# Mixer of a hybrid trunk: x turned on the host, and decay rows spread over the partitions through DRAM

## What is computed

```python
def rms_norm(x, g):
    return x * lax.rsqrt(jnp.mean(x * x, axis=-1, keepdims=True) + RMS_EPS) * g

def attn_ssd_mixer(h, ...):            # h = rms_norm(x, mix_norm_g)
    proj = h @ w_in                    # 1024 x 2312
    q, k, v, z, xbc, dt = split(proj)  # 512, 128, 128, 512, 1024, 8 columns
    q, k = rms_norm(q, q_norm_g), rms_norm(k, k_norm_g)          # by head of 64
    y_attn = sliding_window_sink_attention(q, k, v, sinks)       # window 128, 8 heads
    y_ssm = mamba2_heads(z, xbc, dt, ...)                        # 8 heads
    return concatenate([y_attn, y_ssm]) @ w_out

# inside mamba2_heads: xbc = silu(causal conv of 4 taps), then in chunks of 128 tokens
a_cum = jnp.cumsum(dt * a_coef, axis=2)                 # 128 tokens x 8 heads
seg = a_cum[:, :, :, None] - a_cum[:, :, None, :]       # needs a_cum along both axes
decay = jnp.exp(jnp.where(tril, seg, -jnp.inf))
y_diag = einsum(cb * decay, x * dt)
```

## Time and profile before

| | us |
|---|---|
| three runs | 2082.68, 2100.13, 2100.52 |
| median of them | 2100.13 |
| the profiled execution | 2083.14 |
| its span, first to last instruction | 2081.3 |
| the mixer in it, to the last `project_part` | about 514 |

### The profile page before, as it was taken

How to read it: one execution, slowest core, us unless ns; L and a number is a source line. 1 busy time by engine, 2 the same in 40 slices (tenths; PEclk the granted TensorE clock), 3 DMA queues, 4 the chain that set the end, 5 groups by cost and what they waited for, 6 DMA issues and landing times. The chain is left out here.

```text
span 2081.3 us, 47130 instructions
## 1 busy us (share of the span) xinstructions
PE 1879.5 (90%) x20636; PEld 1153.3 (55%) x20636; DVE 882.7 (42%) x1980; ACT 429.2 (21%) x965; POOL 427.1 (21%) x546
## 2 busy tenths in 40 slices
PE   7899999998699998898969999799969999898992
PEld 5666667664566655555635444345546665555651
DVE  2665565565721111111116899893271111111114
ACT  3332322234311110110114122143411111010110
POOL 2111100111222332222213011120222232221220
PEclk9999999999799999999989999899979999999996
DMA  9100000030699999999968455512289999999996
GB/s 312 37 1 1 1 0 0 0 122 17 254 377 423 422 424 426 425 425 425 421 250 254 100 110 127 121 31 81 81 326 401 416 424 424 428 422 424 423 390 257
DMA packets 89992, 520.60 MB, mean 250 GB/s; under 512 B 23062, under 2 KB 46666, under 8 KB 72384
## 3 DMA queue, kind: packets, MB, share of 16 engines
q1 hardware_dynamic: 63976, 457.76, 53.7%
q0 software_dynamic: 24064, 51.45, 9.0%
q10 hardware_dynamic: 1752, 8.44, 1.0%
HBM read 491.31 MB, written 34.65 MB: 253 GB/s over the span
## 5 line engine op out<-in xcount | busy, mean ns | idle before, releaser
L1367 PE MATMUL ps<-wgu,xT 128*32 128x256 f32 x7168 | 419.0, 387 | 35.1 <-issue 35.1
L1532 DVE TENSOR_TENSOR hh<-sg,ps 128x128 f32<-128x128 f32 x168 | 66.5, 396 | 704.5 <-ACT sg L1189 704.1
L1367 PEld LDWEIGHTS ps<-wgu,xT 128*32 128x32 f32 x7168 | 238.7, 112 | 192.2 <-issue 56.6
L1252 POOL DMA_INDIRECT y_rows<-my,yidx x168 | 166.6, 992 | 736.5 <-ACT my L1183 729.2
L1367 PE MATMUL ps<-early_gu,xT 128*32 128x256 f32 x3584 | 213.3, 392 | 14.9 <-issue 12.3
L1382 PE MATMUL ps<-wd,hhT 128*32 128x256 f32 x3584 | 213.8, 379 | 0.0
L1189 ACT ACTIVATE sg<-ps 128x128 f32<-128x128 f32 x168 | 46.6, 277 | 687.1 <-PE ps L1367 687.1
L1367 PEld LDWEIGHTS ps<-early_gu,xT 128*32 128x32 f32 x3584 | 118.9, 113 | 97.5 <-issue 27.7
L1382 PEld LDWEIGHTS ps<-wd,hhT 128*32 128x32 f32 x3584 | 119.6, 110 | 73.8
L2098 DVE SCALAR_TENSOR_TENSOR conv<-dd,par,conv 128x256 f32<-128x256 f32 (+1 forms) x255 | 131.5, 593 | 0.2
L787 PE MATMUL ps<-hn,early_gu 128*128 128x128 f32 x1024 | 116.8, 275 | 0.0
(11 more groups left out here) (344 smaller groups left out, 2110.9 us busy)
## 6 DMA issues: line engine op xcount, KB each, us to landing
wgu<-in_moe_w_gate_up SPq DMA_DIRECT2D x42, 4096.0 KB, 31.6
early_gu<-in_moe_w_gate_up SPq DMA_DIRECT2D x22, 4096.0 KB, 30.8
wd<-in_moe_w_down SPq DMA_DIRECT2D x42, 2048.0 KB, 29.9
early_wd<-in_moe_w_down SPq DMA_DIRECT2D x22, 2048.0 KB, 29.0
early_wd<-in_conv_w_pw SPq DMA_DIRECT2D x22, 512.0 KB, 5.5
conv<-prod POOLq DMA_DIRECT2D x20, 512.0 KB, 4.5
h_rows<-wgu ACTq DMA_DIRECT2D x8, 1024.0 KB, 3.9
early_gu<-in_w_in SPq DMA_DIRECT2D x2, 2048.0 KB, 16.7
```

What stands on the lines that cost most here:

```text
L1252: pool.indirect_dma_start(out=y_quarters, out_offset=bass.IndirectOffsetOnAxis(ap=yidx[:, tl, q:q + 1], axis=0), in_=y[:, n % YB, :], in_o ...
L1367: mm = pe.matmul(ps[TB * g:TB * g + TB, GU + n % 2, 0:2 * P].rearrange("p (a f) -> p a f", a=2), xT[:, q % 2, j, TB * tl:TB * tl + TB], wg ...
L1532: tt(hh[:, n % 2, :].rearrange("q (k f) -> q k f", k=KF), by_k(sg[:, n % 2, :]), by_k(ps[:, GU + n % 2, P:2 * P]), ALU.mult).then_inc(hh_r ...
```

## The change

- The host passes x turned (`x_turned`, 8 tiles of [128 channels, 8, 128 tokens]) beside x, and the gains and convolution weights already turned (`mixer_rows`). SyncE loads one turned tile (0.5 MB) per turn into `xT`, one buffer.
- For tiles 0 and 1 VectorE multiplies `xT` by the gain (`scale_first`); for tiles 2 to 7 GpSimd does (after `xde`, before `qk_rstd_and_dt`, turns 0 to 5). VectorE's `normalise` multiplies by `rstd` along the free axis, straight from SBUF into `hT`. `turn_hn` and `hT_evacuate` are gone.
- `rstd` along the free axis: for tiles 0 and 1 by a transpose of a repeated column (`turn_rstd`); for tiles 2 to 7 by a store of [128, 6] to DRAM and a load spread over the partitions, for which VectorE waits ahead of turn 0 (`rstd_spread`).
- Decay rows: behind q's and k's transposes TensorE multiplies `a` (stationary) with the triangle (moving), which gives `acum` as 8 rows of 128; VectorE copies them out first in its turn, SyncE stores them (4 KB), waits, and loads them spread over the partitions (512 KB) into `seg`. The 8 transposes are gone; VectorE subtracts within SBUF.
- q's weights come in two transfers, z's ahead of x tile 1, and the router's loads after turn 1's rows. The k/v projection of tile 1 moves behind `xb_turned` as in the other turns.

```diff
@@ sync: loads @@
             sp.dma_start(x[:, 0, :], tiles[:, 0, :]).then_inc(x0_loaded, 16)
-            sp.dma_start(w_in[:, :, Q0:K0], w[:, :, 0:512]).then_inc(wq_loaded, 16)
+            sp.dma_start(xT[:], I["x_turned"][0]).then_inc(xT_loaded, 16)
+            for half in range(2):
+                sp.dma_start(w_q[:, half, :, :], w[:, 4 * half:4 * half + 4, 0:512]).then_inc(wq_loaded[half], 16)
...
+            sp.dma_start(w_z, w[:, :, 768:1280]).then_inc(wz_loaded, 16)
             sp.dma_start(x[:, 1, :], tiles[:, 1, :]).then_inc(x1_loaded, 16)
-            sp.dma_start(w_z, w[:, :, 768:1280]).then_inc(wz_loaded, 16)
+            sp.wait_ge(hT_ready, 2)
+            sp.dma_start(xT[:], I["x_turned"][1]).then_inc(xT_loaded, 16)
...
-            load_router(k, sp, 0)
+            sp.wait_ge(hT_ready, 4)
+            sp.dma_start(xT[:], I["x_turned"][2]).then_inc(xT_loaded, 16)
+            sp.wait_ge(rstd_ready, 3)
+            with nc.allow_non_contiguous_dma(reason="roots by tile"):
+                sp.dma_start(k.rstd_rows.rearrange("n p -> p n")[:, 2:NT], rstd[:, 2:NT]).then_inc(rstd_stored, 16)
+            sp.wait_ge(rstd_stored, 16)
+            sp.dma_start(rstd_rows[:, 2:NT, :].rearrange("p n t -> p (n t)"), k.rstd_rows[2:NT, :].rearrange("n p -> (n p)").partition_broadcast(P)).then_inc(rstd_spread, 16)
+            for c in range(NT):
+                sp.wait_ge(acum_kept, c + 1)
+                sp.dma_start(k.decay_rows[c % 2], acum_T[:]).then_inc(rows_stored, 16)
+                sp.wait_ge(rows_stored, 16 * c + 16)
+                if c:
+                    sp.wait_ge(y_done, c)
+                sp.dma_start(rows[:, :, :].rearrange("p h l -> p (h l)"), k.decay_rows[c % 2].rearrange("h l -> (h l)").partition_broadcast(P)).then_inc(rows_spread, 16)
+                if 1 <= c < NT - 2:
+                    sp.wait_ge(hT_ready, 2 * c + 4)
+                    sp.dma_start(xT[:], I["x_turned"][c + 2]).then_inc(xT_loaded, 16)
+                if c == 1:
+                    load_router(k, sp, 0)
@@ gpsimd: turn @@
                 pool.tensor_tensor(xde[:], xdt[:], se[:, 1, :].unsqueeze(2).to_broadcast([P, NS, DH]), ALU.mult).then_inc(xde_ready, 1)
+                if nxt2:
+                    pool.wait_ge(xT_loaded, 16 * (c + 3))
+                    take_wait()
+                    pool.tensor_tensor(xT[:], xT[:], par[:, :, G_IN:G_IN + 1].to_broadcast([P, KD, P]), ALU.mult).then_inc(xT_scaled, 1)
@@ vector @@
-            def normalise(c, p):
-                dve.tensor_scalar(hn[:, :].unsqueeze(1), x[:, at(c), :], rstd[:, at(c)], None, ALU.mult).then_inc(hn_ready, 1)
+            def scale_first(c):
+                dve.wait_ge(xT_loaded, 16 * c + 16)
+                link(dve.tensor_tensor(xT[:], xT[:], par[:, :, G_IN:G_IN + 1].to_broadcast([P, KD, P]), ALU.mult))
+            def normalise(c, row):
+                for half in range(2):
+                    dve.tensor_tensor(hT[:, 4 * half:4 * half + 4, :], xT[:, 4 * half:4 * half + 4, :], row.to_broadcast([P, 4, P]), ALU.mult).then_inc(hT_ready, 1)
...
+            dve.wait_ge(rstd_spread, 16)
@@ vector: turn @@
-                if nxt and not (isinstance(c, int) and c == 0):
-                    hT_evacuate(c + 1, 1 - p)
                 dve.wait_ge(qk_turned, c + 1)
+                if not (isinstance(c, int) and c == 0):
+                    dve.wait_ge(rows_stored, 16 * c)
+                dve.tensor_copy(acum_T[:], ps[0:NS, S5, 2 * P:3 * P]).then_inc(acum_kept, 1)
...
-                dve.wait_ge(rows_done, c + 1)
...
+                dve.wait_ge(rows_spread, 16 * (c + 1))
+                link(dve.tensor_copy(sm[:, 2, :].unsqueeze(2), rows[:, :, P - 1:P]))
+                for h in range(NS):
+                    dve.tensor_scalar(seg[:, h, :], rows[:, h, :], acum[:, h:h + 1], 0.0, ALU.subtract, ALU.min).then_inc(rows_out, 1)
...
                 if nxt2:
                     dve.wait_ge(x1_projected, c + 2)
-                    normalise(c + 2, p)
+                    dve.wait_ge(xT_scaled, c + 1)
+                    normalise(c + 2, rstd_rows[:, at(c + 2), :])
@@ tensor: turn @@
-                if first:
-                    turn_hn(c + 1, 1 - p)
...
+                pe.wait_ge(a_ready, c + 1)
+                pe.matmul(ps[0:NS, S5, 2 * P:3 * P], a[:], upper[:], start=True, stop=True).then_inc(qk_turned, 1)
...
-                for h in range(NS):
-                    mm = pe.transpose(ps[:, B7 if h < 4 else B6, (h % 4) * P:(h % 4 + 1) * P], acum[:, h:h + 1].to_broadcast([P, P]), ident[:])
-                mm.then_inc(rows_done, 1)
```

More of the change, by code:

```diff
@@ L265, in mixer @@
         seg = sb("seg", [P, NS, P])
+        rows = seg
+        acum_T = sb("acum_T", [NS, P])
         dec = mt = seg
@@ L791, in _, with turn_rstd @@
             pe.wait_ge(ident_ready, 1)
-            pe.wait_ge(rows_loaded, 16 * 9)
-            for j in range(KD):
-                n = ROWS if j < 2 else G_QK
-                mm = pe.transpose(ps[:, S4, j * ROWS:j * ROWS + n], rows[0:n, j * P:(j + 1) * P], ident[0:n, 0:n])
-            mm.then_inc(rows_turned, 1)
-            turn_hn(0, 0)
-            pe.wait_ge(hT_ready, 2)
-            pe.wait_ge(wq_loaded, 16)
-            project(0, 0, PJ0, Q0, K0, q_projected)
+            def turn_rstd(c):
+                pe.wait_ge(rstd_ready, c + 1)
+                pe.transpose(ps[:, B6 + c, 0:P], rstd[:, c:c + 1].to_broadcast([P, P]), ident[:]).then_inc(rstd_turned, 1)
+            turn_rstd(0)
+            for half in range(2):
+                pe.wait_ge(hT_ready, half + 1)
+                pe.wait_ge(wq_loaded[half], 16)
+                for j in range(4 * half, 4 * half + 4):
+                    mm = pe.matmul(ps[:, PJ0, :], hT[:, j, :], w_in[:, j, Q0:K0], start=(j == 0), stop=(j == KD - 1))
+            mm.then_inc(q_projected, 1)
             pe.wait_ge(wkv_loaded, 32)
@@ L805, in _ @@
             project(0, 0, PJ0, Z0, X0, z_projected)
+            turn_rstd(1)
             pe.wait_ge(wx_loaded[0], 16)
@@ L844, in project_out @@
                 pe.wait_ge(yT_ready, c + 1)
-                project_part(c, p, 0, 0, KD)
-                if nxt is not None:
-                    turn_hn(*nxt)
-                project_part(c, p, 1, 0, KD)
+                for half in range(2):
+                    project_part(c, p, half, 0, KD)
             def turn(c, p, nxt, nxt2, it):
                 first, second = isinstance(c, int) and c == 0, isinstance(c, int) and c < 2
-                if first:
-                    turn_hn(c + 1, 1 - p)
                 if not first:
@@ L939, in turn @@
                     pe.wait_ge(x0_out, c + 2)
-                if not first:
-                    if nxt:
-                        pe.wait_ge(y_out, c + 1)
-                        project_out(c - 1, 1 - p, (c + 2, p) if nxt2 else None)
-                elif nxt2:
-                    turn_hn(c + 2, p)
+                if nxt and not first:
+                    pe.wait_ge(y_out, c + 1)
+                    project_out(c - 1, 1 - p)
             turns(pe, turn)
```

101 lines of the change are left out of this document (42 added, 59 removed).

## The result

The kernel after takes 2116.13 us in the median of 4 runs (2113.05 to 2119.13), the kernel before 2097.65 (2082.68 to 2100.52). The ratio is 1.0115, 95% interval 1.0068 to 1.0163: slower by some 1.2%, where +8 us (0.4%) was forecast. A later comparison (experiment 8) gave 2120.2 us against 2102.4, ratio 1.0078 (1.0061 to 1.0095).

A forecast was written before the change was run, and what follows sets the result against it. TensorE's sequence and its wait for VectorE were taken to bound the mixer; 0.7 + 1.1 + 5.4 + 0.2 + 0.4 = +7.8, said +8, on a median of 2100 gave 2108 us, range 2078 to 2120.

The forecast's parts named there:

- The hold: Loop: GpSimd's scaling behind `xde` delays VectorE's L679, for which TensorE waits; 2.0 us a turn, bounds 0 and 2.5.
- main line: Whole kernel: GpSimd's scaling delays L679 with few falls of the clock; likeliest 2108 us, chance 0.45.
- Rival 1: Loop: VectorE gets in ahead of the scaling or only short instructions are held; 2096 us, chance 0.22.
- The loop turn: One turn: +0.22 for `a` times the triangle, -0.87 for `turn_hn`, +2.0 for L679's delay; +1.35 us.
- The transposes costed at 0: Loop: removing the decay transposes (0.97 us) gains nothing, since they lie ahead of TensorE's wait where VectorE paces.
- The start: Ahead of turn 0: x's loads +2.7 us, roots' store 4, load 4, queue 1; first scores +6 us, bounds +0 to +9.
- the nearest row: Roots' store ahead of turn 0: 768 single floats priced from 5.4 us for 1024 single floats; 4 us.
- Turn 0 behind the scores: Turn 0 after its first scores: only the delay of L679 by GpSimd's scaling was added, +2.0 us.
- rival 2: Loop: granted clock falls behind waits from about 3 us, 1.7 us in each of six turns; 2118 us, chance 0.18.
- The turned input: Turn 0's x projection to turn 1's q projection: shorter gap gives 5.5 us, full-clock projection 1.8; 7.3 us back.
- Later stages unchanged: Behind the mixer: what follows starts from its end and keeps its length, so 0 us.

The follow-up runs named there:

- experiment 8: Kernel after, unchanged, run again beside the kernel before on the same chip: 2120.2 us against 2102.4, ratio 1.0078.
- experiment 7: Three unused wide matmuls put on TensorE shortly ahead of the router's first logits, in both kernels: before 2086.1 us, after 2101.1 us.
- experiment 1: Kernel after with GpSimd's scaling of the turned x moved from behind `xde` to the top of its turn: 2105.2 us.
- experiment 4: Kernel after with the decay rows made as before, by 8 transposes on TensorE, the turned x kept: 2120.8 us, measured once.
- Experiment 9: Roots stored as 128 pieces of 24 bytes (outputs wrong), in the kernel after and in a version with every cure: store 7.4 and 2.3 us.
- experiment 5: Kernel before with one spare GpSimd instruction behind `xde`: a `tensor_tensor` gave 2109.9 us (turns 61.70), a `memset` 2097.1 us (turns 60.24).
- experiment 6: Four output projections put ahead of turn 7's wait: kernel before 6 runs at 2096 to 2102, 4 at 2082 to 2088; both cures 2077 to 2096.
- experiments 1 to 3: Kernel after with the scaling moved to the top of GpSimd's turn (2105.2 us), the roots' trip behind turn 0's decay rows (2102.7), or both (2093.3).
- both cures: Kernel after with the scaling at the top of GpSimd's turn and the roots' trip behind turn 0's decay rows: 2093.3 us.
- experiment 2: Kernel after with the roots' store and load issued behind turn 0's decay rows, VectorE waiting for them at turn 0's end: 2102.7 us.

## Where the prediction was right and where wrong

The forecast's terms beside what the profiles show, as the change of each stretch's length in us. The last column is the kernel after against the kernel before, both with experiment 7's matmuls. Turn 0 is counted here to the end of its x projection, since what the turned input gives back begins there.

| | forecast | before to after | in experiment 7 |
|---|---|---|---|
| turn 0, to the end of x's projection | +8.0 | +15.1 | +12.8 |
| from there to turn 2 | -6.2 | -6.5 | -6.5 |
| turns 2 to 5 | +5.4 | +8.7 | +4.1 |
| turn 6 | +0.2 | +0.5 | +0.5 |
| turn 7 | +0.4 | +2.5 | +0.9 |
| sum | +7.8 | +20.2 | +11.8 |

**The hold (main line): right in kind, mis-sized.** Forecast 2.0 us on L679; measured 1.46, in the changed kernel and in the kernel before with a spare instruction. The scaling takes 1.91 us, less than the 2.1 to 2.5 worked out from the earlier trace rows (a product of 1024 elements takes less than twice one of 512), and VectorE's pass is issued 0.30 us behind its start. Rival 1 is refuted.

**The loop turn: +1.08 against +1.35.** Without the hold -0.65 was forecast and -0.38 came (experiment 1): `turn_hn`'s 0.87 us were saved in full, but the product of `a` costs 0.5 and not 0.22. The transposes costed at 0 were worth 0 (experiment 4): of their 0.97 us 0.79 came back as waits for VectorE, 0.40 ahead of the scores and 0.39 more ahead of the probabilities. VectorE's chain from `xb_turned` to L679's end, 13.33 us before, is 13.31 in experiment 1.

**The start, where the forecast failed: every term right but one.** x's projection is out at 52.13, 2.7 us later as forecast; GpSimd's root ends at 56.66 (56.8); the load takes 3.8 us (4); the scores follow VectorE's start by 1.4. The store of single numbers took 10.2 us, forecast 4 and 1 for the queue. The step that failed is the nearest row: 1024 single numbers in 5.4 us were a transfer from DRAM into SBUF, and I took the same price per number for one from SBUF into DRAM. It costs 5 us more here, which is the +10.6 against the forecast +6, and more than the upper bound of +9. Experiment 9 shows that the single numbers make it long; whether it is the direction that makes them dearer than in the load wasn't tried. The Trainium skill (DMA: Bandwidth & Descriptors, Rules for kernel authors) says that such a dimension becomes one descriptor per element; the 784 packets of experiment 9 agree, but the count alone doesn't set the time.

**Turn 0 behind the scores: the clock wasn't in the sum.** Only the hold, +2.0, was put there, and +4.5 came. The hold comes to 0.6 net, since the z projection behind the second scores runs at full clock now (7.13 us, before 8.83). The rest is half clock: 2.3 us between the first scores and the second, behind the 9.43 us that TensorE waits for the roots, and 1.6 in half of x's projection (8.94 us where it took 7.31). The prediction let TensorE wait there and priced the wait only, while rival 2 looked for the clock in the loop.

**The turned input: right.** 7.3 us were given back between turn 0's x projection and the end of turn 1's q projection. They measure 7.1: the gap between the two is 1.5 us where it was 6.9, and the projection takes 7.10 and not 8.80. Of the old gap 1.8 us lay ahead of turn 1's first instruction, so they don't show in turn 1's length, 61.86 us where it was 66.41.

**Rival 2 came true in part, on top of the main line.** It wanted about 3 us of wait as the point from which the clock falls, and put it off at 2.5. At 2.77 it fell in 2 of 5 turns in both profiles of the kernel after (+2.9 and +1.6), and in none in experiment 7's; in turn 0 it fell behind a wait of 2.10. So no such point shows. Turn 7, costed at +0.4, has a wait of 4.05 and not 3.09, and with the half clock behind it costs 2.5, in experiment 7's kernel after, with the same wait, 0.9.

**"Later stages unchanged" was wrong for the profiled executions, and matters little for the medians.** In the profiles the router's stage lasts 30.7 us before and 46.9 after, and that is 16 of the 36 us between them. The medians hold little of it, since 3 of the 4 runs of the kernel before belong to the slower group too. The stage's two lengths, 31 and 46 us, would explain nearly all of the 17 or 18 us between the runs of the kernel before (none of its slower runs was profiled; experiment 5's `memset` and experiment 6 show 46 with the old mixer), which I had noted and put into the range as a spread without a place. The right question at the time was where the execution of 2083 and those of 2100 differ.

**The sum.** Forecast +8 on a median of 2100.13; measured 15.0 us at an equal clock in the router's stage, 17.8 with both at half clock there, 18.5 in the first comparison. By the profiles of experiment 7, of the 4.0 us that the mixer is over the forecast, 4.8 are turn 0 (4 the store, the clock and the hold the rest), 0.9 the last two turns, and 1.7 come off in between, most of it in the loop, where the hold was put too high. That sum is 11.8 and the medians differ by 15.0. The kernel after's profiled execution is the third quickest of its ten, and half clock in some of the loop's turns, which its other profiles show, would fill the difference; which turns fell in the other nine isn't known.

**What stays open.** Why the changed kernels' router stage ran at half clock, by their times, in every run of the first comparison and of experiments 1 to 3, where the kernel before's often didn't, isn't settled. The pause of 1.4 us is the same in both and stays in experiment 7, so it doesn't decide it alone. Turn 7's longer wait was a suspect, but experiment 6 only moved it, and the granted clock was 1.00 from 506 to 536 us, between turn 7's half clock and the stage. In the profile of both cures with the four projections moved TensorE falls to half clock in turn 7 too (the turning of the probabilities takes 1.94 us, not 1.06), and the stage still runs at full clock (31.6 us); so turn 7's fall doesn't decide it either. And what decides in which turns a 2.77 us wait is followed by half clock wasn't tried.

## What to carry to other kernels

Ahead of moving work to GpSimd, look for the VectorE instructions with two SBUF operands that run at that time on the critical chain, and put it where there are none: the same instruction cost 1.46 us a turn in one place and nothing that shows in another. A small store of scattered single numbers isn't small: price it by a row of the same direction and pattern, keep it off the path to the first turn, and look at what lands beside it. Where the sum has an engine wait for long, add what the clock does behind the wait. Where executions of the kernel before differ by more than the effect that is asked for, find the stage in which they differ before forecasting.

## Not expected of the hardware

- 768 numbers of 4 bytes from SBUF to DRAM took 9.2 to 11.3 us over all runs, with and without other traffic; as 128 pieces of 24 bytes 2.3 us without and 7.4 with it. Without other traffic the 784 packets show within 1 us, and the landing came 9 us behind them. A load of 512 KB, issued 0.4 us ahead of such a store, landed with it after 11.5 us, and in 4.2 where the store came later (experiment 2).
- Two short pauses of TensorE (1.8 and 1.4 us) 2 us apart, among narrow matmuls, were followed by the rest of the stage at 1.2 GHz in part of the executions, and, by their times, in none of the 20 (before and after) with three wide matmuls put behind the second: 16 us of 2100 hang on that.
- GpSimd held a VectorE pass of 1.23 us to 2.69 by a product that reads two operands from SBUF; a `memset` of the same length held it by nothing.
